# Two transformer blocks on one core: an earlier start of the modulation chain, and bias tables made ahead of neighbourhood attention

## What is computed

```python
mod = silu(c) @ w_ada + b_ada                  # 6 vectors of 1024: sh1, sc1, g1, sh2, sc2, g2
h = rms_norm(x, norm1_g) * (1 + sc1) + sh1
proj = h @ w_in                                # q, k, v (256 each), c_q 384, c_kv 256, k_rope 32, conv 3*256
y_na = neighbourhood_attention(norm(q), norm(k), v, na_rpb)   # 4 heads, window 8 rows x 16 columns
y_mla = latent_attention(norm(c_q), norm(c_kv), k_rope, ...)  # 8 heads
mixed = group_norm([y_na, y_mla, short_conv(conv)])
x = x + g1 * (mixed @ w_out)
h2 = rms_norm(x, norm2_g) * (1 + sc2) + sh2    # then a gated feed-forward
```

## Time and profile before

| what | value |
|---|---|
| median of 3 runs | 3087.12 us (3082.66 to 3091.01) |
| the profiled execution's own time | 3084.6 us |
| its span | 3083.0 us |
| TensorE matmuls busy | 2920.8 us (95%) |
| VectorE busy | 1776.4 us (58%) |
| ScalarE busy | 1007.5 us (33%) |
| GpSimd busy | 429.6 us (14%) |
| DMA | 257.55 MB, mean 84 GB/s |
| chain that ended last | TensorE 86%, VectorE 8%, ScalarE 2%, issue 2%, DMA 1% |

### The profile page before, as it was taken

How to read it: one execution, slowest core, us unless ns; L and a number is a source line. 1 busy time by engine, 2 the same in 40 slices (tenths; PEclk the granted TensorE clock), 3 DMA queues, 4 the chain that set the end, 5 groups by cost and what they waited for, 6 DMA issues and landing times.

```text
span 3083.0 us, 39822 instructions
## 1 busy us (share of the span) xinstructions
PE 2920.8 (95%) x16215; PEld 2282.2 (74%) x16215; DVE 1776.4 (58%) x1908; ACT 1007.5 (33%) x1307; POOL 429.6 (14%) x464
## 2 busy tenths in 40 slices
PE   2998999999999999999998999999999999999989
PEld 2885666667788888888777888888777876666667
DVE  5556626662445545553487848667654236676783
ACT  2123435552311111111234424334323114454462
POOL 0002010000111111110101103021111002232340
PEclk7999999999999999999999999999999999999999
DMA  6355011011133333331114233243421221212021
GB/s 232 109 171 134 4 28 29 8 29 35 48 103 116 116 116 105 100 101 55 36 48 127 83 89 110 75 137 130 136 104 48 96 96 41 69 35 69 35 74 64
DMA packets 247832, 257.55 MB, mean 84 GB/s; under 512 B 14277, under 2 KB 208674, under 8 KB 247682
## 3 DMA queue, kind: packets, MB, share of 16 engines
q1 hardware_dynamic: 223968, 178.78, 18.9%
q0 software_dynamic: 17680, 58.89, 6.3%
q10 hardware_dynamic: 6034, 17.74, 1.5%
HBM read 222.37 MB, written 30.64 MB: 82 GB/s over the span
## 4 chain that ended last, share of the span: by engine, by line
PE 86%; DVE 8%; ACT 2%; issue 2%; DMA 1%; ACTq 0%; SPq 0%; DVEq 0%
PE PU L994 18%; PE PU L996 18%; PE PU L995 18%; PE PM L1637 2%; PE PU L1615 2%; PE PU L1305 2%; DVE small L2788 2%; PE PM L1657 2%; PE PM L1625 2%; PE PM L1659 2%; PE PM L1658 2%; PE PU L1008 2%; PE PU L1237 1%; PE PU L1009 1%; PE PU L1010 1%
## 5 line engine op out<-in xcount | busy, mean ns | idle before, releaser
L994 PE MATMUL PU<-hH,w_hi_t 128*128 128x512 f32 (+1 forms) x1936 | 764.3, 395 | 4.9 <-DMA hL<-kept_group_low 2.5
L996 PE MATMUL PU<-hH,w_lo_t 128*128 128x512 f32 (+1 forms) x1936 | 755.6, 390 | 0.0
L995 PE MATMUL PU<-hL,w_hi_t 128*128 128x512 f32 (+1 forms) x1936 | 755.0, 390 | 0.0
L994 PEld LDWEIGHTS PU<-hH,w_hi_t 128*128 128x128 f32 (+1 forms) x1936 | 363.4, 188 | 82.6 <-DVE w_lo_t L2380 3.8
L996 PEld LDWEIGHTS PU<-hH,w_lo_t 128*128 128x128 f32 (+1 forms) x1936 | 362.8, 187 | 78.6
L995 PEld LDWEIGHTS PU<-hL,w_hi_t 128*128 128x128 f32 (+1 forms) x1936 | 363.5, 188 | 74.4
L2380 DVE TENSOR_TENSOR w_lo_t<-w_raw,w_hi_t 128x1024 fp32r<-128x1024 f32 x181 | 230.1, 1272 | 301.9 <-ACT w_hi_t L1769 289.8
L1769 ACT ACTIVATE w_hi_t<-w_raw 128x1024 fp32r<-128x1024 f32 x167 | 174.5, 1045 | 440.0 <-PE PU L996 341.0
L2854 DVE SCALAR_TENSOR_TENSOR xT<-PU,mod,xT 128x1024 f32<-128x1024 f32 x120 | 154.0, 1283 | 191.8 <-PE PU L996 191.8
L949 POOL TENSOR_SCALAR_AFFINE_SELECT s_keep<-s_keep 128x128 f32<-128x128 f32 x128 | 114.0, 907 | 504.7 <-ACT s_keep L2268 504.1
L3136 DVE TENSOR_TENSOR_SCAN s_keep<-s_keep,zero 128x128 f32<-128x128 f32 (+7 forms) x128 | 180.6, 1411 | 4.7 <-POOL s_keep L949 4.7
(11 more groups left out here) (417 smaller groups left out, 4836.1 us busy)
## 6 DMA issues: line engine op xcount, KB each, us to landing
ada_w<-in_ada_w_dram POOLq DMA_DIRECT2D x64, 384.0 KB, 4.0
w_raw<-in_w_gu_dram SPq DMA_DIRECT2D x44, 512.0 KB, 3.8
w_raw<-in_m_in_w_dram SPq DMA_DIRECT2D x40, 512.0 KB, 3.9
ada_w<-in_w_ada_dram POOLq DMA_DIRECT2D x32, 512.0 KB, 4.6
seg<-decay_sums SPq DMA_DIRECT2D x32, 512.0 KB, 4.4
w_raw<-in_w_down_dram SPq DMA_DIRECT2D x22, 512.0 KB, 3.4
w_raw<-in_w_in_dram SPq DMA_DIRECT2D x17, 512.0 KB, 3.8
ada_w<-in_w_ada_dram SPq DMA_DIRECT2D x16, 512.0 KB, 18.6
```

Of the source, the lines that this page charges most:

```text
L994: mm(PU[0:width, up, half, :], whi, aH[:, k, cols], start=k == 0, stop=False)
L995: mm(PU[0:width, up, half, :], whi, aL[:, k, cols], start=False, stop=False)
L996: last = mm(PU[0:width, up, half, :], wlo, aH[:, k, cols], start=False, stop=k == kt - 1)
```

## The change

1. c and c_2 leave the parameter rows and go, first on ACT's queue, into a tile `c_stage` of their own; TensorE turns it before x, and ScalarE makes silu(c) from PSUM. The 34 other rows are issued by POOL after its constants; TensorE turns them after x. ScalarE copies all eight x tiles; VectorE none. VectorE starts the first chain after silu(c), and copies `vec` and inverts x's root between the two chains. `rope_inv` is issued by ACT behind the x tiles.
2. The write of `bias_rows` moves behind the second slab that POOL fetches in the projections.
3. The bias table is two tiles: heads 0 and 1 in the place of `w_raw`, loaded once all projection panels are split; heads 2 and 3 in hH's place, loaded as before. The split of the first w_out panel moves to head unit 4 (ScalarE) and 5 (VectorE), and SP loads the two first w_out panels after norm rows 4 to 6 and after step 7's logits.
4. Masking and the inner copy are two functions. The first masking stands before the steps, the inner copy after step 0; folding krope's squares after step 1, scaling c_kv after step 2, the second norm's gains after step 3, the second masking after step 5 and its copy after step 6. Root and inverse of krope's norm come after the steps; ACT issues the positions in step 4.

```diff
-for _name, _n in (("m_conv_w_2", 96), ("m_norm_g_2", 16), ("c", 8), ("c_2", 8)):
+for _name, _n in (("m_conv_w_2", 96), ("m_norm_g_2", 16)):
...
+        c_stage = at("c_stage", A + 8704, [2 * KD, P])
...
-        b2 = at("b2", H, [P, NAH, 16, GRID])
+        b2 = [at("b2_first", 8192, [P, 2, 16, GRID]), at("b2_second", H + 2048, [P, 2, 16, GRID])]
...
# SP
+            for e in range(4, 7):
+                norm_rows(e)
+            sp.wait_ge(na_l, 2 * TT)
             for t in range(2):
                 panel(w_out[:, :, t * P:(t + 1) * P], KD, P)
-                norm_rows(4 + t)
-            norm_rows(6)
...
# GpSimd
+            g.wait_ge(vec_done, 1)
+            for name, src, rows, width in VEC_ROWS(a):
+                g.dma_start(v_stage[c % P:c % P + rows, c // P, 0:width], src).then_inc(vec_dma, 16)
+            for name, src, off, width in VEC_PARTS(a):
+                g.dma_start(v_stage[c % P:c % P + 1, c // P, off:off + width], src).then_inc(vec_dma, 16)
...
-            g.wait_ge(rp_landed, 16)
-            g.dma_start(scr_bias, rp[0:nrow, :].unsqueeze(1).broadcast_to([nrow, GRID, P])).then_inc(rp_landed, 16)
...
+                    if slab.n == 2:
+                        g.wait_ge(rp_landed, 16)
+                        g.dma_start(scr_bias, rp[0:nrow, :].unsqueeze(1).broadcast_to([nrow, GRID, P])).then_inc(rp_landed, 16)
             g.wait_ge(rp_landed, 32)
-            g.wait_ge(unit_done[1], len(WIN_UNITS) // 2)
+            for p in range(2):
+                g.wait_ge(w_split[p], len(WIN_UNITS) // 2)
             for hh in range(NAH):
+                if hh == 2:
+                    g.wait_ge(unit_done[1], len(WIN_UNITS) // 2)
...
# TensorE
-            pe.wait_ge(vec_dma, 16 * N_VEC_DMA)
-            for n in range(NVEC):
-                last = nc.tensor.transpose(PM[:, 2, n * P:(n + 1) * P], v_stage[:, n, :], ident[:, :])
-            last.then_inc(vec_t, 1)
+            pe.wait_ge(rope_dma, 32)
+            nc.tensor.transpose(PM[:, 3, 0:2 * KD], c_stage[:, :], ident[0:2 * KD, 0:2 * KD]).then_inc(vec_t, 1)
             for t in range(TT):
...
+            pe.wait_ge(vec_dma, 16 * N_VEC_DMA)
+            for n in range(NVEC):
+                last = nc.tensor.transpose(PM[:, 2, n * P:(n + 1) * P], v_stage[:, n, :], ident[:, :])
+            last.then_inc(vec_t, 1)
+            spread(rt[:, 0, :])
             pe.wait_ge(cact_done, 1)
-            spread(rt[:, 0, :])
+            pe.wait_ge(vec_done, 2)
...
# ScalarE
+            for n, name in enumerate(("c", "c_2")):
+                act.dma_start(c_stage[n * KD:(n + 1) * KD, :], a[name].rearrange("o (r c) -> (o r) c", c=P)).then_inc(rope_dma, 16)
+            act.wait_ge(vec_t, 1)
+            af(cact[:, :], PM[:, 3, 0:2 * KD], ACT.Silu).then_inc(cact_done, 1)
...
                 if n:
-                    split()
+                    if kind != "krope":
+                        split()
...
-                    norm_root(len(NORMS) - 1)
-                    act.dma_start(pos[:, :], a["positions"].broadcast_to([P, T])).then_inc(rope_dma, 16)
...
+                if s == 4:
+                    act.wait_ge(sq_fold, len(FOLDS))
+                    act.dma_start(pos[:, :], a["positions"].broadcast_to([P, T])).then_inc(rope_dma, 16)
+            norm_root(len(NORMS) - 1)
...
+                if n == 4:
+                    split()
...
# VectorE
-            model_inverse()
             for b in range(2):
+                if b:
+                    ve.wait_ge(vec_t, 2)
+                    V.tensor_copy(vec[:, :], PM[:, 2, 0:NVEC * P]).then_inc(vec_done, 1)
+                    model_inverse()
...
-            squares_folded(len(FOLDS) - 1)
-            norm_applied(NORMS.index(("ckv", 1)))
-            norm_inverse(len(NORMS) - 1)
...
+            def after_step(s):
+                if s == 0:
+                    na_inner(0)
+                if s == 1:
+                    squares_folded(len(FOLDS) - 1)
+                if s == 2:
+                    norm_applied(NORMS.index(("ckv", 1)))
+                if s == 3:
+                    ve.wait_ge(ada_mod, 6)
+                    gains(coef[:, 1, :], m("sc2", 0, 8), v("norm2_g", 0, 8))
+                if s == 5:
+                    na_masked(1)
+                if s == 6:
+                    na_inner(1)
+            ve.wait_ge(w_split[0], len(WIN_UNITS) // 2)
+            ve.wait_ge(w_split[1], len(WIN_UNITS) // 2)
+            na_masked(0)
+            ada_finish([(40, VEC["b_ada"][0] + 40, 8)])
...
+            norm_inverse(len(NORMS) - 1)
...
+                if n == 5:
+                    split()
```

More of the change, by code:

```diff
@@ L2483, in _ @@
                 link(V.memset(small[r0:r0 + ROPE // 2, 1:2], -1.0))
-            ve.wait_ge(vec_t, 1)
-            V.tensor_copy(vec[:, :], PM[:, 2, 0:NVEC * P]).then_inc(vec_done, 1)
-            for t in range(1, TT, 2):
-                ve.wait_ge(x_t, t + 1)
-                V.tensor_copy(xT[:, :, t * P:(t + 1) * P], PU[:, 1, :, :].rearrange("p a (b q) -> p (a b) q", q=P))\
-                    .then_inc(x_ev[1], 1)
-            ve.wait_ge(vec_done, 2)
             ve.wait_ge(cact_done, 1)
@@ L2506, in _ @@
                 ada_reduced(ada_w[:, b, :], ada_acc2[:, b, :], b)
+            ve.wait_ge(vec_done, 2)
             for b in range(2):
@@ L2552, in _ @@
                     squares_folded(FOLDS.index(WIN_UNITS[n - 1][0:2]))
-                if n:
+                if n and kind != "krope":
                     split()
@@ L2584, in _, with na_masked @@
                     skip()
-            squares_folded(len(FOLDS) - 1)
-            norm_applied(NORMS.index(("ckv", 1)))
-            norm_inverse(len(NORMS) - 1)
-            ada_finish([(40, VEC["b_ada"][0] + 40, 8)])
-            ve.wait_ge(ada_mod, 6)
-            gains(coef[:, 1, :], m("sc2", 0, 8), v("norm2_g", 0, 8))
             V.memset(g_sum[:, MIX_PLACE[6]:MIX_PLACE[7] + 1, :, :], 1.0)
-            V.memset(b2[0:64, :, 15, :], 0.0)
-            link(V.memset(b2[64:128, :, 0, :], 0.0))
-            def na_tables(i):
+            def na_masked(i):
+                V.memset(b2[i][0:64, :, 15, :], 0.0)
+                link(V.memset(b2[i][64:128, :, 0, :], 0.0))
                 ve.wait_ge(b2_landed[i], 64)
-                for hh_ in (2 * i, 2 * i + 1):
-                    rows = b2[:, hh_, :, :]
+                for hh_ in range(2):
+                    rows = b2[i][:, hh_, :, :]
                     ins = V.scalar_tensor_tensor(rows, rows, -1.0, na_mask[:, :].unsqueeze(1).broadcast_to([P, 16, GRID]),
@@ L2621, in _ @@
                             d0 = NA_PAIRS[pair][1]
-                            bias = b2[:, 2 * i + hd, d0:d0 + 8, :].rearrange("p r w -> p (r w)")
+                            bias = b2[i][:, hd, d0:d0 + 8, :].rearrange("p r w -> p (r w)")
                         ve.wait_ge(na_s, s + 1)
@@ L3208, in _ @@
             out_scaled(TT - 1)
-N_VEC_DMA = 36
+N_VEC_DMA = 34
 def VEC_ROWS(a):
@@ L3235, in VEC_ROWS @@
     yield "m_norm_g_2", rows(a["m_norm_g_2"]), 16, P
-    yield "c", rows(a["c"]), 8, P
-    yield "c_2", rows(a["c_2"]), 8, P
     yield "dt_bias", a["m_dt_bias_2"], 1, NH
```

52 lines of the change are left out of this document (22 added, 30 removed).

## The result

| | before | after |
|---|---|---|
| median | 3087.6 us (3082.66 to 3091.01, 4 runs) | 3056.46 us (3055.49 to 3057.73, 4 runs) |
| profiled execution, its span | 3084.6, 3083.0 us | 3057.7, 3056.1 us |
| TensorE matmuls, VectorE, ScalarE, GpSimd busy | 2920.8, 1776.4, 1007.5, 429.6 us | 2920.6, 1770.9, 1012.3, 447.6 us |

The ratio is 0.9898 (95% interval 0.9883 to 0.9914): 31 us off. The forecast was 3062, so the change won 5.5 us more than I said. TensorE does the same work; what went is its idle time at the two places.

The account below looks back on a forecast made before the run. A VectorE chain was taken to bound the beginning, VectorE's work and late table loads the border; 15.9 + 8.0 = 23.9 us off 3084.6 gives 3060.7, or 3063.2 from the median; forecast 3062, range 3052 to 3072.

Parts of the forecast that it names:

- Silu(c): Beginning: c lands by about 8.5 us; after a transpose, table load and activation, silu(c) is ready near 11.
- The rows: Beginning: 34 parameter rows on POOL's queue at 0.5 us an issue, issued by 21.3 and landed by 27.4.
- Rival A: Beginning: parameter rows come late; at 0.85 us an issue the last lands at 39.3, 5.7 late: 3068; chance 0.12.
- the lock: Beginning: VectorE's two-port operations hold back POOL's row issues until the first chain ends, 7.1 us late: 3069; chance 0.03.
- Slabs: Beginning: weight slabs let the first chain start at 20.5, slabs 4 to 7 land at 25.9; beginning gains 15.9 us.
- The border before the first logits: Projections to attention: early table and moved VectorE work bring first logits near 278.2 for 288.16, a gain of 9.9 us.
- The steps: Attention steps 0 to 7: 32.8 us undisturbed plus one clock fall of 3.7, 36.5, a loss of 1.9 us.
- Rival B: Attention steps: TensorE keeps its clock through the shorter pauses, 3.7 us better, 3058; chance 0.17.
- The absorption: Attention steps: VectorE has slack of 1.1 us a step, so 9.0 us of added work costs 4.6.
- Rival C: Attention steps give the gain back by a second clock fall, unabsorbed work or both: 3066 to 3070; chance 0.10.
- D: Beginning: every parameter-row issue on POOL costs 1.68 us, the second chain begins 33.9 late: slower, 3095; chance 0.02.
- E: Beginning: the start does not move, held by something unseen; only the border gain is left: 3078; chance 0.04.

Follow-up runs that it names:

- the run with the rows on its queue: Changed kernel with the 34 parameter rows issued from ScalarE's queue behind c and c_2 instead of POOL's; 3056.29 us, ratio 0.9903.
- the run with the rows twice: Changed kernel with each of the 34 parameter rows loaded twice by POOL, TensorE turning them only when all 68 are there; 3068.41 us, ratio 0.9944.
- the run with the norm work ahead: Changed kernel with the last fold and ckv scaling on VectorE ahead of step 0 instead of after steps 1 and 2; 3063.19 us, ratio 0.9931.
- the beginning alone: Kernel before with only the new beginning and the later bias write, the border as it was; 3066.89 us, ratio 0.994.
- the run with one piece: Changed kernel with the second masking and its inner copy in one block after step 3 instead of after steps 5 and 6; 3056.4 us, ratio 0.9906.
- the border alone: Kernel before with only the new border (two-tile table, norm work between steps, w_out split in the head phase), old beginning; 3073.89 us, ratio 0.9961.
- the late table: Changed kernel with the first half of the bias table loaded only when the krope unit is done; 3067.75 us, ratio 0.9947.
- the run with the busy VectorE: Changed kernel with 18 unused copies within SBUF on VectorE from about 6.5 us on, where it was idle; 3058.03 us, ratio 0.9913.

## Why the prediction was right, and where its sizes were off

The mechanism held at both places, and 3056.5 lies in the range. Working through its own steps:

- **Silu(c)** came at 6.33, forecast near 11: c was there at 6.04, 4.2 us behind the end of its two issues, where I had taken 8.5 from the rpb read, and the table load stood at 1.90, before c, hidden. **The root** came at 24.44 for 30.6: 4.7 us by the earlier silu(c), the rest because the rope_inv issues (21.37) ran beside the last copy of x and not behind it. Neither is on the path; that the root can come 8.3 us later was shown by the run with the rows on its queue.
- **The rows**: 0.48 to 0.55 us each as taken, but for the first two (1.22 together) and one of 0.74; last issue at 21.39, turned at 26.89 for 27.4. Rival A and the lock did not decide. That late rows would have, and at the price I gave, the run with the rows twice shows: one us for one us. It also shows the lock as I had read it to be wrong: its second 34 rows went out at 0.48 to 0.54 each through the whole first chain.
- **Slabs**: first 20.07 for 20.5, wait to 25.42 for 25.9; the second chain never waited, as said. The start gained 16.7 where I had 15.9. That 16.7 was also my upper bound is chance: I had it for a first chain that waits for no slab, and it did wait; the 0.8 more came mostly from slabs 0.4 to 0.5 earlier and from `vec` and reciprocal taking 0.57 for 0.8. The "slabs 12 to 15 landing at 36.8" never mattered; my lower bound, slabs at 42, was the bias write's old cost, and it would have been paid in the first chain.
- **The border before the first logits**: 10.5 for 9.9, and 0.3 more from the projections. The first logits stand 2.3 us behind the unit where I had 2.8: masking with its memsets took 2.8 for 3.0, and began before the unit had ended (257.49).
- **The steps** are the mis-sized term. Undisturbed I had 32.8 and they took 32.21; but I added one clock fall of 3.7, took a loss of 1.9, and it was a gain of 2.4. This 4.3 us is most of the error. The price was wrong too. I had put all of the 3.7 down to the one fall behind the masking and overlooked that the steps had begun at half clock. Steps 0 to 2 lasted 10.47 us in the kernel before; in the run with the norm work ahead, which has the same work there and the inner copy hidden besides, they lasted 9.88, of which 0.93 were a slow step 0. So some 1.5 of the 3.7 was the slow beginning and some 2.2 the fall behind the masking (an estimate from these rows). The changed kernel has neither, the first because TensorE no longer stands 12 us ahead of the steps. Rival B, to which I gave 0.17, is what happened. Its argument ("each new pause is under 2 us") stood in the text and weighed too little; the runs show the fall to go with the one long piece of VectorE work: it is there in the kernel before, in the beginning alone and in the run with one piece, and absent in the border alone and in all but one of the others. Why it came once in the new order is open.
- **The absorption** of 1.1 us a step held for steps 1 and 2: of 5.0 us between the steps 2.3 were absorbed.
- **The head phase** cost nothing, as said. **Sum**: 16.7 + 0.3 + 10.5 + 2.4 = 29.9 for 23.9.
- Going from the profiled execution to the median I took 3062, between 3060.7 and 3063.2; as the profiled execution of before lay 2.5 low, 3063.2 was the number to give.

Rival C did not come, D and E are excluded by the issues at 0.48 and by the beginning alone. Not settled: how much a clock fall costs. Behind VectorE's work it was some 2.2 in the kernel before, at most 1.4 in the run with one piece and 1.6 in step 7 of the rows twice; at the start of the steps, behind a stand of 9 us, it was 0.9 with the norm work ahead and 1.5 with the late table.

## What to carry to other kernels

When a start is fed by one queue at full bandwidth, list everything that shares the bandwidth before the last needed byte, and move out what is needed late: here one 1.97 MB write was worth 7 of the 16.7 us, once the engines no longer waited for something else. Take work out of the way of a waiting engine by cutting it into pieces that fit between its steps; here the clock then also stayed up, in eight of nine profiles. When time is left over in a sum, look at the granted clock of every stretch before putting it down to one. And after each such gain look at what the engines do right behind the old bottleneck: a short operation queued behind a long one that nobody needs yet (0.40 us behind 3.78) ate most of the gain here: 1.1 us was left of 4.8.

## What the runs showed of the hardware

VectorE holds GpSimd up in two different ways. An operation with one source in SBUF (copy, TENSOR_SCALAR) holds GpSimd's DMA issue until it ends: 0.74 for 0.48 us, and, in the run with the busy VectorE, 19 issues in a row at the pace of the operations. Multiply-adds with two SBUF sources leave issues alone, but hold GpSimd's own computing; of the kernel after, GpSimd's order of time:

```profile
20.18 0.74 POOL L818 DMA_DIRECT2D v_stage<-in_mla_kr_g_dram  x1
...
22.22 0.21 POOL L825 TENSOR_SCALAR_AFFINE_SELECT na_mask<-na_mask 64x48 f32<-64x48 f32 x1
22.58 1.02 POOL L827 TENSOR_SCALAR_AFFINE_SELECT na_mask<-na_mask 64x48 f32<-64x48 f32 x1
23.75 1.18 POOL L825 TENSOR_SCALAR_AFFINE_SELECT na_mask<-na_mask 64x48 f32<-64x48 f32 x1
```

The selects take 0.21 us alone and 1.02 to 1.18 beside multiply-adds of 1.3 us. The Trainium skill, SBUF — State Buffer, "SBUF: two separate sides", says just that: an exclusive lock for the whole operation, against descriptor writing for a two-port operation, and for one with two SBUF inputs only against a GpSimd operation that reads SBUF. I had read it as holding the rows until the whole chain ends; by the runs only the chain's first operation holds one, for 0.26 us.

An issue of a small row cost 0.27 us on ScalarE's queue and 0.48 on GpSimd's. And a transfer was there 3.3 us (the last row, in the run with the rows twice) to 4.0 us (the late table) behind the end of its issue, away from the opening load, and 5.0 (the last row of the kernel after) to 5.4 (the rpb read of the earlier trace rows) beside it.
